# The FFN down projection of a two-layer decoder by seven block products instead of eight, with the decay mask folded into its exponential

## The reference, cut to what matters

```python
x = x + 0.5 * swiglu(rmsnorm(x, norm_ffn1[l]), w1_gate[l], w1_up[l], w1_down[l])
# mixer: h @ w_in, differential attention (4 heads), retention (4 heads), concat @ w_out, added to x
x = x + 0.5 * swiglu(rmsnorm(x, norm_ffn2[l]), w2_gate[l], w2_up[l], w2_down[l])

def swiglu(x, w_gate, w_up, w_down):
    return (silu(x @ w_gate) * (x @ w_up)) @ w_down      # 1024 -> 2816 -> 1024
# retention's mask: intra = where(rel >= 0, exp(log_decay * rel), 0); keys are scaled by 64 ** -0.5
```

## Time and profile before

| what | us |
|---|---|
| median of 3 runs | 964.54 (963.11 to 965.75) |
| the profiled execution, its own time | 965.07 |
| its span, first to last instruction | 963.0 |
| PE busy | 948.3 (98%) |
| DVE busy | 555.4 (58%) |
| ACT busy | 458.8 (48%) |
| POOL busy | 208.8 (22%) |
| weights and other data read from memory | 173.96 MB |

### The profile page before, as it was taken

One profiled execution on the slowest core, in us unless ns is written; L12 is line 12 of the kernel. 1 busy time (PEld: TensorE's weight loads), 2 busy tenths in 40 slices (PEclk: granted clock), 3 DMA queues, 4 the chain that ended last, 5 costly groups with the idle time before them and its releaser, 6 DMA issues.

```text
span 963.0 us, 12593 instructions
## 1 busy us (share of the span) xinstructions
PE 948.3 (98%) x4379; PEld 783.8 (81%) x4379; DVE 555.4 (58%) x623; ACT 458.8 (48%) x580; POOL 208.8 (22%) x237
## 2 busy tenths in 40 slices
PE   8999999999999999999999999999999999999997
PEld 7788888888888888888887888888888887888885
DVE  5555565666575555455665555556665755555554
ACT  6444444465564454444444444444556445444442
POOL 4543321000010332221024212110001024322210
PEclk9999999999999999999999999999999999999999
DMA  8788676735353887676746867664624647867651
GB/s 281 204 202 254 208 229 195 247 126 167 111 178 128 221 232 232 190 228 196 247 106 195 269 191 224 192 222 151 224 83 175 218 118 200 271 187 220 195 163 44
DMA packets 166051, 185.98 MB, mean 193 GB/s; under 512 B 49264, under 2 KB 139424, under 8 KB 166016
## 3 DMA queue, kind: packets, MB, share of 16 engines
q1 hardware_dynamic: 122080, 174.09, 55.1%
q10 hardware_dynamic: 43616, 10.52, 6.5%
q0 software_dynamic: 320, 0.92, 0.7%
HBM read 173.96 MB, written 1.05 MB: 182 GB/s over the span
## 4 chain that ended last, share of the span: by engine, by line
PE 89%; DMA 3%; ACT 2%; DVE 2%; POOL 2%; issue 1%; SPq 1%; ACTq 0%; POOLq 0%; DVEq 0%
PE gu L868 19%; PE gu L870 19%; PE gu L869 19%; PE acc L868 9%; PE acc L870 9%; PE acc L869 9%; DMA kT<-kT 2%; ACT w_hi L358 1%; DVE w_lo L594 1%; PE tp L1004 1%; DMA raw<-in_w_up_dram 1%; PE tp L886 1%; POOL kT L258 1%; PE acc L1015 1%; PE tp L1027 1%
## 5 line engine op out<-in xcount | busy, mean ns | idle before, releaser
L594 DVE TENSOR_TENSOR w_lo<-raw,w_hi 128x2048 fp32r<-128x2048 f32 (+1 forms) x164 | 373.0, 2278 | 156.8 <-ACT w_hi L358 156.8
L868 PE MATMUL gu<-w_hi,xT_hi 128*128 128x512 f32 x892 | 350.2, 393 | 3.8 <-DVE w_lo L594 2.7
L870 PE MATMUL gu<-w_hi,xT_lo 128*128 128x512 f32 x892 | 347.4, 389 | 0.0
L869 PE MATMUL gu<-w_lo,xT_hi 128*128 128x512 f32 x892 | 347.2, 389 | 0.0
L358 ACT ACTIVATE w_hi<-raw 128x2048 fp32r<-128x2048 f32 (+1 forms) x164 | 305.5, 1866 | 15.1 <-DMA raw<-in_w_in_dram 7.2
L868 PEld LDWEIGHTS gu<-w_hi,xT_hi 128*128 128x128 f32 x892 | 167.5, 188 | 40.6 <-DVE w_lo L594 4.9
L870 PEld LDWEIGHTS gu<-w_hi,xT_lo 128*128 128x128 f32 x892 | 167.4, 188 | 35.2
L869 PEld LDWEIGHTS gu<-w_lo,xT_hi 128*128 128x128 f32 x892 | 167.5, 188 | 33.9
L868 PE MATMUL acc<-w_hi,aT_hi 128*128 128x512 f32 x384 | 150.8, 393 | 0.7 <-DVE aT_lo L623 0.7
L870 PE MATMUL acc<-w_hi,aT_lo 128*128 128x512 f32 x384 | 149.7, 390 | 0.0
L869 PE MATMUL acc<-w_lo,aT_hi 128*128 128x512 f32 x384 | 149.5, 389 | 0.0
(11 more groups left out here) (129 smaller groups left out, 436.8 us busy)
## 6 DMA issues: line engine op xcount, KB each, us to landing
raw<-in_w_down_dram SPq DMA_DIRECT2D x88, 512.0 KB, 4.1
raw<-in_w_gate_dram SPq DMA_DIRECT2D x84, 512.0 KB, 4.1
raw<-in_w_up_dram SPq DMA_DIRECT2D x84, 512.0 KB, 5.0
raw<-in_w_in_dram SPq DMA_DIRECT2D x40, 512.0 KB, 4.7
raw<-in_w_out_dram SPq DMA_DIRECT2D x16, 512.0 KB, 4.1
raw<-in_w_in_dram SPq DMA_DIRECT2D x16, 256.0 KB, 3.0
raw<-in_w_gate_dram SPq DMA_DIRECT2D x8, 256.0 KB, 4.0
raw<-in_w_up_dram SPq DMA_DIRECT2D x8, 256.0 KB, 5.5
```

The source lines that it names most:

```text
L594: nc.vector.tensor_tensor(w_lo[:, pos % SLOTS, 0:n], raw[:, pos % RAW, 0:n], w_hi[:, pos % SLOTS, 0:n].bitcast(F32), ALU.subtract).then_in ...
L868: nc.tensor.matmul(out_, s_hi, m_hi, start=first, stop=False)
L869: nc.tensor.matmul(out_, s_hi, m_lo, start=False, stop=False)
L870: return nc.tensor.matmul(out_, s_lo, m_hi, start=False, stop=last)
```

## The change

1. **Down projection of the first ten steps of each FFN.** The hidden part of a step, 256 x 256, is seen as 2 x 2 blocks of 128 x 128 (a11, a12, a21, a22) and the weight piece, 256 x 1024, as 2 x 2 blocks of 128 x 512 (b11 to b22). Seven block products of sums of blocks take the place of eight products of the blocks (Strassen's scheme, in the form with few sums). Six of them add up over the steps in PSUM (four `acc` banks and the two `tp` banks); the seventh, a12 b21, goes to the bank of `gu` that is free and DVE adds it to x in each step (`read_p2`). The eleventh step stays in the plain form.
2. **The sums.** POOL makes four sums of weight blocks, 128 x 512 each (`weight_sums`), DVE four sums of hidden blocks, 128 x 128 each (`hidden_sums`). What has to be split into hi and lo for a down piece is now three blocks of the piece (1536 columns) and the four sums (2048 columns), and for the hidden three blocks and four sums (896 columns).
3. **Slots.** Of the six slots one holds a down piece's blocks (`BASE_AREA`), one its sums (`SUM_AREA`), four the up pieces. So a down piece can be split only when PE is done with the down before it. The first two pieces of the next stage take such places; the second of them waits for the last product that reads them.
4. **The end.** The banks in `acc` and `tp` are put together by ACT, DVE (p16, p167, p5) and three sums on POOL (`spread`). In the last step `ahead_after(..., [1])` stands behind `last_lo(banks[1], 1)`.
5. **The mask.** The distances above the diagonal are set to 3.0e38 before the exponential (an `affine_select` on POOL, ahead of the making of the bias), and the scale comes in as the exponential's bias; the scaling and the second `affine_select` go.

In the diff below, comments name the engine a part belongs to, and the conditions that skip a part in an FFN's first step are left out.

```diff
+            def weight_sums(f, s_, which):                      # POOL
+                if which == 0:
+                    pool.wait_ge(raw_loaded[pos % RAW], 32 * (LP // RAW * layer + pos // RAW + 1))
+                    pool.wait_ge(sum_lo_done, n)
+                    nc.gpsimd.tensor_tensor(t1, b12, b11, ALU.subtract).then_inc(w_sums, 1)
+                    nc.gpsimd.tensor_tensor(t3, b22, b12, ALU.subtract).then_inc(w_sums, 1)
+                else:
...
+                    nc.gpsimd.tensor_tensor(t2, b22, t1, ALU.subtract).then_inc(w_sums, 1)
+                    nc.gpsimd.tensor_tensor(t4, b21, t2, ALU.subtract).then_inc(w_sums, 1)
+            def step(f, s_):
+                turn_out(f, s_, 0)
+                weight_sums(f, s_, 0)
+                turn_out(f, s_, 1)
+                weight_sums(f, s_, 1)
+                for tt in range(TT):
+                    turn_back(f, s_, tt)
...
+                def down_hi(n, it, pos):                        # ACT
+                    act.wait_ge(slot_free, LP * layer + SLOTS * it + base + pos + 1 + RAW)
+                    nc.scalar.activation(w_hi[:, BASE_AREA, 0:512], piece[:, 0:512], ACT.Copy).then_inc(base_hi_done, 1)
+                    nc.scalar.activation(w_hi[:, BASE_AREA, 512:1536], piece[:, 1024:2048], ACT.Copy).then_inc(base_hi_done, 1)
+                    act.wait_ge(w_sums, 4 * n + 4)
+                    nc.scalar.activation(w_hi[:, SUM_AREA, :], mix[:, :, :].rearrange("p i n -> p (i n)"), ACT.Copy).then_inc(hi_done, 1)
+                def step(s_, n, banks, it, pos, lots):          # ACT
+                    down_hi(n - 1, it, lots[0])
+                    silu(s_, 0, it, pos, banks)
+                    turned_hi(n - 1)
+                    split_hi(layer, base + lots[1], it)
+                    turn(2 * n, 0)
+                    silu(s_, 1, it, pos, banks)
+                    split_hi(layer, base + lots[2], it)
+                    turn(2 * n + 1, 1)
...
+                def step(e, n, m, banks, it, lots, guard=True): # DVE
+                    down_lo(n - 1, it, lots[0])                 # 512, 1024, 2048 columns; lo_done after the 1024
+                    hidden_sums(n - 1)                          # 4 x (128 x 128)
+                    hide(e, 0, banks, 2 * n - 1 if guard else None)
+                    turned_lo(n - 1)                            # 256, 128, 512 columns
+                    split_lo(layer, base + lots[1], it)
+                    hide(e + 1, 1, banks, 2 * n if guard else None)
+                    read_p2(m, banks[0])
+                    split_lo(layer, base + lots[2], it)
+                def last_step(e, n, banks):                     # DVE
...
+                    last_lo(banks[0], 0)
+                    nc.vector.scalar_tensor_tensor(p16, tp[0][:, :], 0.5, p1_half, ALU.mult, ALU.add).then_inc(p16_done, 1)
+                    nc.vector.scalar_tensor_tensor(p167, tp[1][:, :], 0.5, p16, ALU.mult, ALU.add).then_inc(p167_done, 1)
+                    nc.vector.scalar_tensor_tensor(x[:, 0, 512:1024], acc[3][:, :], 0.5, x[:, 0, 512:1024], ALU.mult, ALU.add).then_inc(p5_read, 1)
+                    ahead_after(layer, f, [0])
+                    last_lo(banks[1], 1)
+                    ahead_after(layer, f, [1])
...
+                def down(n, m, it, pos, bank, used, first=False):   # PE: 7 blocks x three
+                    block(bank, 1, BASE_AREA, 1, True, True).then_inc(p2_ready, 1)
+                    block(acc[0], 0, BASE_AREA, 0, first)
+                    block(tp[0], 4, SUM_AREA, 1, first)
+                    block(tp[1], 5, SUM_AREA, 2, first)
+                    block(acc[3], 3, SUM_AREA, 0, first)
+                    block(acc[2], 2, SUM_AREA, 3, first)
+                    block(acc[1], 6, BASE_AREA, 2, first).then_inc(slot_free, 1)
...
+                block(acc[2], 2, SUM_AREA, 3, False).then_inc(slot_free, 1)   # the end
+                add_rows(layer, 0, 1, base + end + 3, endT_hi, endT_lo, 0, last=True, halves=[0])
+                    enter_T(q + 1, 0)
+                add_rows(layer, 0, 1, base + end + 3, endT_hi, endT_lo, 0, last=True, halves=[1], on=True)
...
-            nc.gpsimd.tensor_scalar(decay[:, :, :], decay[:, :, :], SCALE, None, ALU.mult).then_inc(pool_steps, 1)
...
-                nc.scalar.activation(decay[:, h, :], decay[:, h, :], ACT.Exp, scale=LOG_DECAY[h]).then_inc(decay_exp, 1)
+                nc.scalar.activation(decay[:, h, :], decay[:, h, :], ACT.Exp, bias=log_scale, scale=LOG_DECAY[h]).then_inc(decay_exp, 1)
```

More of the change, by code:

```diff
@@ new lines, in step, with spread @@
+            def step(f, s_):
[3 more added lines that the diff above has]
+                weight_sums(f, s_, 1)
+                for tt in range(TT):
+                    turn_back(f, s_, tt)
+            def spread(f):
+                for i, (when, rows, src) in enumerate(((p16_done, (0, 1), p16), (p167_done, (1, 0), p167), (p167_done, (1, 1), p167))):
+                    tt, half = rows
+                    part = x[:, tt, half * 512:(half + 1) * 512]
+                    pool.wait_ge(when, f + 1)
+                    if i == 0:
+                        pool.wait_ge(p5_read, f + 1)
+                    nc.gpsimd.tensor_tensor(part, src, part, ALU.add).then_inc(x_summed, 1)
@@ L283, in _, with ffn @@
+            def ffn(layer, half):
+                f = 2 * layer + half
+                for s_ in range(0 if f else 5, STEPS - 1):
+                    step(f, s_)
+                spread(f)
             nc.gpsimd.memset(ident[:, :], 0.0).then_inc(pool_steps, 1)
@@ L302, in _ @@
                 entry(0, tt)
[L303 to L310 removed]
+            step(0, 0)
+            step(0, 1)
+            step(0, 2)
             for i, lam in enumerate((lam_q1, lam_k1, lam_q2, lam_k2)):
@@ new lines, in last_step @@
+                def last_step(s_, n, banks, pos):
+                    down_hi(n - 1, 0, FFN_PIECES - 2)
+                    silu(s_, 0, 0, pos, banks)
+                    turned_hi(n - 1)
+                    split_hi(layer, base + FFN_PIECES - 1)
+                    silu(s_, 1, 0, pos, banks)
+                    last_hi(banks[0], 0)
+                    act.wait_ge(p1_ready, i + 1)
+                    nc.scalar.activation(p1_half, acc[0][:, :], ACT.Copy, scale=0.5).then_inc(p1_read, 1)
+                    ahead_after(layer, f, [0])
+                    last_hi(banks[1], 1)
+                    ahead_after(layer, f, [1])
@@ L925, in project, with add_rows @@
                     ins.then_inc(ready, 1)
-            def add_rows(layer, it, tt, pos, src_hi, src_lo, k0, first=False, last=False):
+            def add_rows(layer, it, tt, pos, src_hi, src_lo, k0, first=False, last=False, halves=range(2), on=False):
                 if tt == 0:
                     piece_ready(layer, pos, it)
-                slot = pos % SLOTS
-                for half in range(2):
+                slot = PHYS[pos % SLOTS]
+                for half in halves:
                     for k in range(2):
@@ L963, in ffn, with block @@
-                up(e0, 0, 0, 0, lambda: enter_T(q, 1), guard=False, entry=q)
-                up(e0 + 1, 0, 0, 1, guard=False, entry=q)
-                up(e0 + 2, 0, 2, 0)
-                up(e0 + 3, 0, 2, 1)
-                for tt in range(TT):
-                    down((dT_lo_done, d0 + tt + 1), 0, 4, 0, tt, first=True)
+                def block(out_, a, area, b, first, last=False, on=False):
+                    cs, ts = slice(b * 512, (b + 1) * 512), slice(a * P, (a + 1) * P)
+                    return three(out_[:, :], a_hi[:, ts], a_lo[:, ts], w_hi[:, area, cs], w_lo[:, area, cs], first, last, on)
@@ new lines, in ffn @@
+                hidden_T(e + 1, 1, gu[0])
+                block(acc[1], 6, BASE_AREA, 2, False)
+                pe.wait_ge(p1_read, i + 1)
+                block(acc[0], 1, BASE_AREA, 1, False, False, True)
+                pe.wait_ge(hT_lo_done, 2 * i + 1)
+                for half in range(2):
+                    add_rows(layer, 0, 0, base + end + 3, endT_hi, endT_lo, 0, last=True, halves=[half], on=half == 0)
+                block(acc[2], 2, SUM_AREA, 3, False).then_inc(slot_free, 1)
+                pe.wait_ge(hT_lo_done, 2 * i + 2)
```

338 lines of the change are left out of this document (185 added, 153 removed).

## The result

The changed kernel takes 1058.76 us (median of 4 runs, 1058.43 to 1059.85), the kernel before 963.83 in the same comparison. The ratio is 1.0982, with a 95% interval of 1.0964 to 1.1000. The profiled execution took 1059.85 us, its span 1057.9.

The account below looks back on a forecast made before the run. PE, busy 98%, bounds the kernel before; after, DVE and POOL excluding each other at a shared SBUF port set the step. 965.07 + 53 (steps) + 18 (FFN ends) = 1036 us, mask zero; range 975 to 1080.

Parts of the forecast that it names:

- The step: One FFN step of an up and a down: 17.8 us, against PE's 16.32 before; 53 us lost over 36 periods.
- the mechanism named: POOL's work and DVE's two-input SBUF operations exclude each other: 10.4 plus 6.7, 17.1 us a step, plus 0.35 at each hide.
- The case against it: POOL holds the gate more briefly, as one residue row hints; PE sets 15.64 us steps: 959 (chance 0.11) or 938 (0.05).
- the count of steps: Nine up-and-down periods per FFN, 36 in all, lose time; each FFN's first up has no down beside it and stays.
- The ends: End of each FFN: next stage 6 us later at three ends, 0 at the fourth; 18 us in all.
- T: At an FFN's end, the time at which the last step's first up is ready; 178.2 before the change.
- The mask: ACT's exponentials at the start run 1.2 us later, covered by 1.1 us: zero cost, at most 1.2 us if uncovered.
- the likeliest case's own range: Whole kernel at 1015 to 1060 us, with steps of 17.2 to 18.4 us; chance 0.62.

Follow-up runs that it names:

- the run with ramps: Changed kernel with plain DMA for the hidden halves; POOL writes ramps reading nothing from SBUF instead of its sums, except each FFN's first step: 980.02 us.
- the control: Changed kernel with the transposing DMA of the hidden halves replaced by a plain DMA of the same bytes: 1053.18 us, ratio 1.0946.
- the experiment: Changed kernel with plain DMA; in the last step, the last block reading the sums moved ahead of the plain rows of tt = 0: 1051.81 us.
- the control of the kernel before: Kernel before the change with the transposing DMA of the hidden halves replaced by a plain DMA of the same bytes: 964.76 us, ratio 1.0024.
- the run with more matmuls: Changed kernel with plain DMA and six more matmuls of 512 columns ahead of each down: 1055.88 us, ratio 1.0932.

## Why the prediction was right, and what it missed

The changed kernel's trace, against that of before, parts the 95 us of its span as follows. The steps are set against PE's pace before, 16.32 us: the silus of that kernel come 16.02 us apart on average, since its first ones are late while PE goes on.

| where | forecast | measured |
|---|---|---|
| steps from each FFN's third silu on | 32 x 1.48 = 47 | 32 x 1.54 = 49 |
| the steps before that | 4 x 1.48 = 6 | 28 |
| ends of the FFNs | 18 | 17 |
| mask and start, until the first silu | 0 | 1 |
| sum | 71 | 95 |

**The step.** Forecast 17.8 us, measured 17.86, by the mechanism named. The price of POOL's subtraction, 1.31 us from two short rows, is what the trace shows for one that waits for nobody (1.30, 119.38 above). The case against it was the row in which DVE got in 0.9 us after the start of a 2.78 us operation on POOL. The Trainium skill (SBUF — State Buffer, "SBUF: two separate sides") has the lock held for the full instruction; for the sums the trace agrees, as the split delayed by 0.48 behind 119.38 and the 512 columns at 122.76 end within 0.15 us of where that rule puts them (120.68 + 2.29 and 123.99 + 0.69; measured 122.83 and 124.54). The same section limits this to GpSimd operations that read SBUF, and the run with ramps agrees: 2300 ns for a split.

**The step of the working that failed is the count of steps.** It said that the first up of an FFN "has no down beside it and stays". The first down was priced like the others. It is not like them: only one up of PE's work lies between the first step's hidden and the wait for it. The timeline of PE at the first down of the second FFN, and POOL ahead of it:

```profile
357.10 0.76 PE L964 MATMUL gu<-w_hi,a_hi 128*128 128x512 f32 x1 [6.00 <-DVE a_lo L675]
```

```profile
339.23 2.60 POOL L273 COPY kT<-hid 128x512 uint16<-128x512 uint16 x1 [3.67 <-DVE hid L719]
341.80 1.31 POOL L292 TENSOR_TENSOR mix<-raw 128x512 f32<-128x512 f32 x1
...
349.03 3.67 POOL L280 COPY qT<-kT 128x512 uint16<-128x512 uint16 x2 [1.44 <-DMA kT<-kT]
```

POOL's first turn_out waits for a split, then come the two sums, the other half, two more sums, the DMA and the turn_backs until 352.7. Only then may DVE form the hidden sums and ACT and DVE split them, while PE stands for 6.0 us. At the four first downs PE waits 5.0, 6.0, 5.0 and 6.6 us, 22.6 in all. The downs behind these waits then take 6.9 to 7.8 us, at granted clocks of 0.60 to 0.69, where 21 matmuls at 0.2267 us need 4.76. In the control this wait of the second FFN is 4.6 us, and so it is where the sums are left out of all later steps. No run took the sums out of the first step alone; with all sums on DVE the four waits are still 3.4 to 3.7 us. How much of the wait POOL's sums make stays open. By the table this term is 22 us over the forecast, nearly all of its error.

**The ends.** Forecast: the next stage starts at T + 23.6 with PE waiting 5 us. Measured at the first end, with T = 197.9, in the timelines of DVE and of PE, to be laid beside the earlier trace rows:

```profile
214.07 2.96 DVE L646 TENSOR_TENSOR w_lo<-raw,w_hi 128x2048 fp32r<-128x2048 f32 x1 [2.47 <-ACT w_hi L399]
...
217.09 1.27 DVE L687 SCALAR_TENSOR_TENSOR x<-acc,x 128x512 f32<-128x512 f32 x2
```

```profile
217.82 1.71 PE L982 MATMUL tp<-ident,x 128*128 128x128 f32 x8 [4.42 <-DVE x L687]
219.19 0.78 PE L964 MATMUL acc<-w_hi,a_hi 128*128 128x512 f32 x1
...
221.78 0.40 PE L964 MATMUL gu<-w_hi,xT_hi 128*128 128x512 f32 x1
```

The split ahead starts at T + 16.2, x is new at T + 20.5, the next stage starts at T + 23.9, PE waits 4.4 us. By the time from the last silu to the second transposes of x the three ends are 6.2, 6.0 and 5.3 us longer; the fourth, to the last instruction, is 0.6 shorter. The size was right (the working's own terms for the way from x to the next stage add up to T + 23.4, not 23.6). Of its cause I named two parts, the late place for the second piece and POOL's sums at the port; the experiment shows that taking away the first alone gives little, since DVE then meets the second. A third part wasn't in the forecast: PE comes back from its wait at the lower clock (below).

**The mask.** ACT's exponentials now run from 3.81 to 5.51, and ACT is next wanted at 7.40: free, as forecast. The first silu starts at 22.72, before at 21.61; in the control, which starts with the same code, it starts at 21.39, so this 1 us isn't shown to be the mask's. The mask was not run by itself.

**Smaller marks.** PE's share is 91%, not 86 to 88, partly because matmuls at the lower clock count as longer busy. The sums' mean over all four is 1.94 us, not 2 or more. PE was to idle 2.2 us a step; from each FFN's third silu on it waits 1.4 us in the mean and loses most of the rest at the lower clock behind the waits. The time lies in the likeliest case's own range, 1 us inside its upper edge. That is luck in part: this range was made for steps of 17.2 to 18.4 us, and 22 us of what fills it come from a term that the working didn't have.

**What stays open.** The steps differ (15.7 to 20.6 us from the third silu on, around their mean), and which order the turns fall into from step to step wasn't traced. The row against a hold for the full instruction isn't explained: the control of the kernel before has it again (the scaling from 34.58 takes 2.78 us, the residue from 35.12 only 0.78), and no run tests such an operation beside a longer split. A version that beats the kernel before was not found. With the port out of the way the changed kernel was still at 977: by its trace the 32 shorter steps give back 22 us, and the ends cost 14 and the time ahead of the FFNs' third silus 20. Both would have to go as well.

## What to carry to other kernels

When work is taken from the full engine and given to two others, don't ask only whether each has room; look for rows in which the two overlap, and whether either is longer there than alone. If they take turns, their work adds up as on one engine: 10.4 us on DVE and 6.7 on POOL fitted singly into 15.6 and together set the step. And price the first and the last round of a pipeline by themselves, since a chain that a full step hides is bare in them.

## What the runs showed of the hardware

- An operation on POOL that writes SBUF but reads nothing from it (a ramp of 1344 columns, 1.27 us) doesn't hold up a DVE operation with two SBUF inputs, nor is it held up. A copy of 16-bit values and a float32 subtraction, which read, do both (turns at 119.38 to 124.46). A DVE copy within SBUF with a single input, 128x128 float32, was held up too, 1.28 us instead of 0.21.
- A float32 subtraction of 128x512 on POOL takes 1.30 us alone, nearly twice DVE's 0.68.
- TensorE's granted clock, 0.998 over the span before, was 0.963 in the changed kernel, whose PE waits 1.4 us in the mean, and up to 3.6, ahead of the later downs. At the first end, after a wait of 4.4 us, eight transposes take 1.71 us, not 1.03, and the last six matmuls of the FFN 2.6 us (219.19 to 221.78), not 1.4. The granted clock of these 4 us is 0.57, so the 1.2 GHz level for most of them, some 1.7 us lost. Inside the later steps the clock cost nothing that the run with more matmuls could win back. Where the port doesn't set the pace it does cost: with the sums left out the first downs still take 6.5 to 7.6 us instead of 4.76, and the periods behind them 17.3 to 18.5 instead of 15.64.
